# Decay matrices two slots ahead in three buffers, and four further changes to the state-space stage of a hybrid diffusion backbone

## What is computed

```python
z, xs, B, C, dt = proj(h)                     # xs, B, C through a 3-tap convolution and silu
# per group (8), per chunk of 128 tokens (10), for both directions:
decay = exp(where(tri, a_cum[l] - a_cum[s], -inf))
y_diag = einsum((C @ B.T) * decay, x * dt)    # inside a chunk
state  = state * chunk_decay + B.T @ (decay_out * x * dt)
y_off  = exp(a_cum) * (C @ state_before)      # from the chunks before
y = (y_f + y_b + x * d_skip) * silu(z)
y = y * rsqrt(mean(y*y over the group) + eps) * norm_g
out = y @ w_out
```

## Time and profile before

| | |
|---|---|
| Median of 3 runs | 2400.05 us (2393.45 to 2405.62) |
| The profiled execution | 2396.67 us, span 2394.9 us |
| PE busy | 2136.1 us (89%) |
| DVE busy | 1425.8 us (60%) |
| ACT busy | 1131.6 us (47%) |
| POOL busy | 463.8 us (19%) |
| Granted TensorE clock, mean | 0.938 |
| `sg_rowb<-crows` DMAs | 80 of 512 KB, median 3.8 us from issue to landing |
| `h_wr<-in_w_ssd` DMAs | 48 of 512 KB, median 3.3 us |

### The profile page before, as it was taken

One profiled execution on the slowest core, in us unless ns is written; L12 is line 12 of the kernel. 1 busy time (PEld: TensorE's weight loads), 2 busy tenths in 40 slices (PEclk: granted clock), 3 DMA queues, 4 the chain that ended last, 5 costly groups with the idle time before them and its releaser, 6 DMA issues. The chain is left out here.

```text
span 2394.9 us, 35742 instructions
## 1 busy us (share of the span) xinstructions
PE 2136.1 (89%) x12490; PEld 1751.9 (73%) x12490; DVE 1425.8 (60%) x3348; ACT 1131.6 (47%) x2840; POOL 463.8 (19%) x449
## 2 busy tenths in 40 slices
PE   5699999899999989999876899569999999999787
PEld 2488777787877878787655788457778778877676
DVE  5475959778695977869395221433545554554652
ACT  5245647465563746556363111324444444444431
POOL 1013223232322323232120000111101111110300
PEclk9899999999999999999877999679999999999899
DMA  9423222131212213121126433321112111211432
GB/s 363 191 65 84 71 87 80 45 103 51 92 54 79 80 44 99 52 96 63 41 75 229 120 115 109 111 72 48 50 45 71 54 50 57 68 50 44 144 77 80
DMA packets 119645, 209.94 MB, mean 88 GB/s; under 512 B 28700, under 2 KB 78876, under 8 KB 117420
## 3 DMA queue, kind: packets, MB, share of 16 engines
q1 hardware_dynamic: 119468, 207.66, 27.1%
HBM read 180.93 MB, written 28.65 MB: 88 GB/s over the span
## 5 line engine op out<-in xcount | busy, mean ns | idle before, releaser
L546 PE MATMUL sg_pP<-h_h_hi,h_whi 128*128 128x512 f32 (+1 forms) x1152 | 438.6, 381 | 0.0
L547 PE MATMUL sg_pP<-h_h_lo,h_whi 128*128 128x512 f32 (+1 forms) x1152 | 415.6, 361 | 0.0
L548 PE MATMUL sg_pP<-h_h_hi,h_wlo 128*128 128x512 f32 (+1 forms) x1152 | 413.6, 359 | 0.0
L546 PE MATMUL at_pP<-h_h_hi,at_whi 128*128 128x512 f32 (+1 forms) x640 | 253.9, 397 | 12.8 <-POOL at_wlo L2084 12.8
L546 PEld LDWEIGHTS sg_pP<-h_h_hi,h_whi 128*128 128x128 f32 x1152 | 226.2, 196 | 30.6 <-issue 0.2
L547 PEld LDWEIGHTS sg_pP<-h_h_lo,h_whi 128*128 128x128 f32 x1152 | 225.8, 196 | 30.4
L548 PEld LDWEIGHTS sg_pP<-h_h_hi,h_wlo 128*128 128x128 f32 x1152 | 224.3, 195 | 32.2
L548 PE MATMUL at_pP<-h_h_hi,at_wlo 128*128 128x512 f32 (+1 forms) x640 | 238.6, 373 | 0.0
L547 PE MATMUL at_pP<-h_h_lo,at_whi 128*128 128x512 f32 (+1 forms) x640 | 237.0, 370 | 0.0
L967 ACT ACTIVATE sg_S<-sg_rowb,sg_tab 128x128 f32<-128x128 f32 x640 | 195.7, 391 | 47.8 <-DVE sg_E L1229 47.8
L2084 POOL TENSOR_TENSOR at_wlo<-at_wr,at_whi 128x1024 fp32r<-128x1024 f32 x32 | 76.3, 2385 | 564.3 <-ACT at_whi L1959 564.3
(11 more groups left out here) (293 smaller groups left out, 4595.4 us busy)
## 6 DMA issues: line engine op xcount, KB each, us to landing
sg_rowb<-crows SPq DMA_DIRECT2D x80, 512.0 KB, 3.8
h_wr<-in_w_ssd SPq DMA_DIRECT2D x48, 512.0 KB, 3.3
fs_w<-in_ada_w SPq DMA_DIRECT2D x16, 1024.0 KB, 8.8
at_wr<-in_w_na SPq DMA_DIRECT2D x32, 512.0 KB, 3.5
at_bias<-bt SPq DMA_DIRECT2D x256, 64.0 KB, 2.3
op_yr<-y SPq DMA_DIRECT2D x10, 1024.0 KB, 7.7
fs_w<-in_ada_w SPq DMA_DIRECT2D x16, 512.0 KB, 8.6
y<-sg_Z SPq DMA_DIRECT2D x16, 512.0 KB, 3.0
```

The lines of the kernel that those rows point to most:

```text
L546: pe.matmul(out, w_hi[:, k, :], h_hi[:, k, t0:t0 + n], start=(k == 0), stop=False)
L547: pe.matmul(out, w_hi[:, k, :], h_lo[:, k, t0:t0 + n], start=False, stop=False)
L548: x = pe.matmul(out, w_lo[:, k, :], h_hi[:, k, t0:t0 + n], start=False, stop=(k == KT - 1))
```

## The change

1. C B^T goes into a bank of its own (`pA[1]`), and DVE makes both masked copies of it from PSUM in the backward slot of the chunk (`masks`, into `cbl` and `cbg`). ACT's copy into `cb` and DVE's `triangles` in later slots are gone.
2. `norm_g` is no longer multiplied onto y in `norm_early` but onto the output weights in `out_project`, in the two instructions that split them; the last step of the norm is one multiplication over both tiles.
3. PE makes `back(g + 1, 0)` in slot 19 of group g, ahead of `forth_inner`; in a slot from 2 on without a unit, `back_state` is put off until behind the next `back`. DVE's `norm_late` in slots 0 and 1 stands ahead of `back`.
4. `rowb` has one buffer instead of two (and so one semaphore, `rld`); the cumulative rows `cumt` are kept in `hb`, `bias` and `alog` in `sq`. A broadcast waits for the `segments` of the chunk before, and the lists of broadcasts are cut otherwise: chunk 0 alone, 1 to 3, 4 to 6, 7 to 9 instead of 0 and 1, 2 to 4, 5 to 7, 8 and 9.
5. `E` has three buffers, and `forward_part`, `masked`, `times_decay` and `decays` work on chunk c + 2 instead of c + 1, `segments` and `nearer` on chunk c + 3 instead of c + 2.

```diff
@@ SP
             def rows(g, chunks):
                 for c in chunks:
                     n = g * NCH + c
-                    if n >= 2:
-                        sp.wait_ge(sgs, n - 1)
+                    if n:
+                        sp.wait_ge(sgs, n)
                     else:
                         sp.wait_ge(rst, 16 * 2 * G)
-                    sp.dma_start(rowb[:, n % 2, :, :].rearrange("p h l -> p (h l)"),
-                                 rows_dram[g, c].rearrange("h l -> (h l)").partition_broadcast(P)
-                                 ).then_inc(rld[n % 2], 16)
+                    sp.dma_start(rowb[:, :, :].rearrange("p h l -> p (h l)"),
+                                 rows_dram[g, c].rearrange("h l -> (h l)").partition_broadcast(P)).then_inc(rld, 16)
...
                 if kind == "x" and g and i:
-                    rows(g - 1, ((0, 1), (2, 3, 4), (5, 6, 7))[i - 1])
+                    rows(g - 1, ((0,), (1, 2, 3), (4, 5, 6))[i - 1])
                 if kind == "x" and g >= 2 and i == 0:
-                    rows(g - 2, (8, 9))
+                    rows(g - 2, (7, 8, 9))
                 if kind == "x" and g == G - 1 and i == XT - 1:
-                    rows(g - 1, (8, 9))
+                    rows(g - 1, (7, 8, 9))
@@ PE
+                if n:
+                    pe.wait_ge(msk, n)
+                pe.matmul(pA[1][:, 0:P], X[:, g % 2, B_, u0:u0 + P], X[:, g % 2, C_, u0:u0 + P],
+                          start=True, stop=True).then_inc(tC, 1)
                 for t in range(XT - 1):
-                    pe.transpose(pT[:, t * P:(t + 1) * P], X[:, g % 2, t, u0:u0 + P], ident[:, :])
-                pe.matmul(pT[:, 3 * P:4 * P], X[:, g % 2, B_, u0:u0 + P], X[:, g % 2, C_, u0:u0 + P],
-                          start=True, stop=True).then_inc(tA, 1)
+                    x = pe.transpose(pT[:, t * P:(t + 1) * P], X[:, g % 2, t, u0:u0 + P], ident[:, :])
+                x.then_inc(tA, 1)
...
+            back(0, 0)
             for g in range(G):
+                behind = None
                 for i in range(NCH):
-                    back(g, i)
+                    if i:
+                        back(g, i)
+                    if behind is not None:
+                        back_state(g, behind)
+                        behind = None
                     if units[g][i] is not None:
                         unit(units[g][i])
-                    if i < NCH - 1:
+                    elif 2 <= i < NCH - 1:
+                        behind = i
+                    if i < NCH - 1 and behind is None:
                         back_state(g, i)
...
+                    if c == NCH - 1 and g + 1 < G:
+                        back(g + 1, 0)
                     forth_inner(g, c)
@@ ACT
-                    if -1 <= c < NCH - 1:
-                        forward_part(g, c + 1)
                     if -2 <= c < NCH - 2:
-                        segments(g, c + 2)
-                    if -1 <= c < NCH - 1:
-                        decays(g, c + 1)
+                        forward_part(g, c + 2)
+                    if -3 <= c < NCH - 3:
+                        segments(g, c + 3)
+                    if -2 <= c < NCH - 2:
+                        decays(g, c + 2)
@@ DVE
-                if g == 0 and nxt == 3:
+                if g == 0 and nxt == 8:
+                    dve.wait_ge(rst, 16 * 2 * G)
                     dve.wait_ge(tst, 32)
...
-            def triangles(g, c):
...
+            def masks(g, i):
+
+                n = g * NCH + i
+                dve.wait_ge(tC, n + 1)
+                if g and i == 0:
+                    dve.wait_ge(wfw, g * NCH)
+                dve.tensor_tensor(cbg[:, BACK[i], :], pA[1][:, 0:P], ge[:, :], ALU.mult)
+                dve.tensor_tensor(cbl[:, BACK[i], :], pA[1][:, 0:P], le[:, :], ALU.mult).then_inc(msk, 1)
...
-                    for t in range(PAIRS):
-                        zt = Z[:, t, (c - 3) * P:(c - 2) * P]
-                        x = dve.scalar_tensor_tensor(zt, zt, ng[:, g * PAIRS + t:g * PAIRS + t + 1],
-                                                     norm_bank(c - 1)[:, P:2 * P], ALU.mult, ALU.mult)
-                    x.then_inc(fin, 1)
+                    zc = Z[:, :, (c - 3) * P:(c - 2) * P]
+                    dve.tensor_tensor(zc, norm_bank(c - 1)[:, P:2 * P].unsqueeze(1).to_broadcast([P, PAIRS, P]), zc,
+                                      ALU.mult).then_inc(fin, 1)
...
+                    if g and s < 2:
+                        norm_late(g - 1, NCH + s)
                     if c >= 0:
                         norm_early(g, c)
                     if c < 0:
+                        masks(g, s)
                         back(g, s)
                     else:
                         offs(g, c)
                         scan(g, c)
-                    if g and s < 2:
-                        norm_late(g - 1, NCH + s)
                     if c >= 0:
                         norm_late(g, c)
-                    if -1 <= c < NCH - 1:
-                        masked(g, c + 1)
-                        times_decay(g, c + 1)
                     if -2 <= c < NCH - 2:
-                        triangles(g, c + 2)
+                        masked(g, c + 2)
+                        times_decay(g, c + 2)
...
-                    if -2 <= c < NCH - 2:
-                        nearer(g, c + 2)
+                    if -3 <= c < NCH - 3:
+                        nearer(g, c + 3)
@@ out_project, for each of the 16 weight tiles (and a load of ng ahead of them)
+                    act.activation(whi[:, k, :], wr[:, k % RW, :], ACT.Copy, scale=ng[:, k:k + 1]).then_inc(whs, 1)
...
+                    dve.scalar_tensor_tensor(wlo[:, k, :], wr[:, k % RW, :], ng[:, k:k + 1],
+                                             whi[:, k, :].bitcast(F32), ALU.mult, ALU.subtract).then_inc(wls, 1)
```

More of the change, by code:

```diff
@@ L618, in ssd_groups @@
         diag = m.sb("diag", [P, P])
-        rowb = m.sb("rowb", [P, 2, H8, P])
+        rowb = m.sb("rowb", [P, H8, P])
         S = m.sb("S", [P, H8, P])
-        E = m.sb("E", [P, 2, HPG, P])
+        E = m.sb("E", [P, 3, HPG, P])
         W = m.sb("W", [P, HPG, P])
@@ L638, in ssd_groups @@
         ecum, dec, dtdec, ncum = tv, te, tu, tq
-        cumt = rowb[0:H2, :, :, :].rearrange("p i h l -> p (i h l)")[:, 0:TOK]
+        cumt = hb[0:H2, :, :].rearrange("p c n -> p (c n)")[:, 4 * UN:4 * UN + TOK]
         GT = TABS * NCH * H8
@@ L698, in _ @@
             load(1)
-            for dst, src in ((par, "conv"), (ng, "norm_g"), (ident, "ident"), (le, "m_le"),
+            for dst, src in ((par, "conv"), (ident, "ident"), (le, "m_le"),
                              (ge, "m_ge")):
@@ L858, in norms @@
                     x.then_inc(ssm, 1)
-            pe.wait_ge(small, 128)
+            pe.wait_ge(small, 112)
             for c in range(NCH):
@@ L966, in segments @@
                 for k in range(H8):
-                    x = act.activation(S[:, k, :], rowb[:, n % 2, k, :], ACT.Identity,
+                    x = act.activation(S[:, k, :], rowb[:, k, :], ACT.Identity,
                                        bias=tab[:, g % 2, NCUM, c, k:k + 1])
@@ L976, in back @@
                 act.activation(X[:, g % 2, 0:XT - 1, u0:u0 + P], pT[:, 0:3 * P].rearrange("p (t c) -> p t c", c=P),
[L977 to L981, removed]
+                               ACT.Copy).then_inc(evA, 1)
             def forward_part(g, c):
                 n = g * NCH + c
-                act.wait_ge(tri, 2 * n + 2)
+                act.wait_ge(msk, masks_of(g, c))
                 if n:
@@ L989, in forward_part @@
                 for k in range(HPG):
-                    x = act.activation(W[:, k, :], cb[:, c, :], ACT.Copy, scale=tab[:, g % 2, DT, c, k:k + 1])
+                    x = act.activation(W[:, k, :], cbl[:, c, :], ACT.Copy, scale=tab[:, g % 2, DT, c, k:k + 1])
                 x.then_inc(wfw, 1)
@@ L995, in decays @@
                 act.wait_ge(mns, n + 1)
-                act.activation(E[:, n % 2, :, :], E[:, n % 2, :, :], ACT.Exp).then_inc(ex, 1)
+                act.activation(E[:, n % 3, :, :], E[:, n % 3, :, :], ACT.Exp).then_inc(ex, 1)
             def square(g, c):
@@ L1081, in _ @@
             pool.wait_ge(con, 5)
-            pool.wait_ge(small, 128)
+            pool.wait_ge(small, 112)
             def scaled(slot, g, c, lo):
@@ L1144, in _ @@
             dve.memset(hz, 0.0).then_inc(con, 1)
-            dve.wait_ge(small, 128)
+            dve.wait_ge(small, 112)
             dve.wait_ge(ttr, 1)
@@ L1395, in _, with out_project @@
                 norm_late(G - 1, c)
-def out_project(nc, a, layer, y_dram, kt, w_dram, tiles, mod_rows, st_o, runs=None):
+def out_project(nc, a, layer, y_dram, kt, w_dram, tiles, mod_rows, st_o, runs=None, scale=None):
     NH = D // 2
@@ L1426, in out_project @@
         N = len(tiles)
+        if scale is not None:
+            ng = m.sb("ng", [P, kt])
+            ngl = m.sem("ngl")
         if runs:
```

(11 more changed lines are left out.)

48 lines of the change are left out of this document (22 added, 26 removed).

## The result

The changed kernel takes **2454.98 us** (median of 4 runs, 2449.44 to 2467.41), the kernel before 2398.28 (4 runs, 2393.45 to 2405.62): ratio 1.024, 95% interval 1.0199 to 1.0281. It is slower, as forecast (2450, range 2405 to 2485). The profiled execution of after took 2459.85 us at a span of 2458.1; before it was 2396.67 at 2394.9. So 63.2 us of span are to be explained.

A forecast was written before the change was run, and what follows sets the result against it. DVE bounds the forward half, PE the backward half. Group 0 +25, groups 1 to 5 +7.0 each, group 6 +2, group 7 -9, output stage +0.5: +53.5 us on 2396.7, so 2450 us, range 2405 to 2485.

The forecast's parts named there:

- The loop: Forward half, group 3: rows wait for segments, loads for ACT's split; PE 11.3 us late at slot 12.
- The cause: Row transfers through the single `rowb` buffer: segments follow segments no faster than 6.2 us.
- Group 0: Eight gather DMAs between load and broadcasts cost 5.3 us three times, 16; with the rest +25 us (17 to 29).
- Slot 3: Backward half: the state product, put off, waits for DVE's masks; between 1.4 us won and 1 lost, taken as 0.6 lost.
- Group 7: No loads in its forward half, slots near 6.2 us; backward half gives 3; -9 us (-11 to -6).
- the steps moved out and the last slots: Group 7's forward half: a gain of 3 us, beside 3.1 from shorter slots.
- What follows the stage: Output stage: 16 splits with a scalar operand and a small load added, +0.5 us (0 to 2).
- (a): Rival: the stall never reaches PE and DVE's relief counts in full, 2335 us; 8%.
- (b): Rival: lateness of the first three broadcasts is absorbed, stalls in slots 11 and 14 remain, 3.7 us each; 2384 us; 10%.
- (c): Rival: PE's lower clock spreads, two to four more slow slots in each of eight groups; 2476 to 2501 us; 10%.
- What was to show it: Profile signs: ACT waits for rows, PE for `sq`, DVE for decays; `L837`'s 39 us mostly go; forward halves 88 to 92.

The follow-up runs named there:

- e1: The changed kernel with the row transfers behind the weight loads in the lists of before (0-1, 2-4, 5-7, 8-9): 2356.62 us, 0.9817 to the kernel before.
- e4: The changed kernel with the extra slot of lead taken back on ACT and DVE, its new lists and one buffer kept: 2354.83 us, 0.9811.
- e2: The changed kernel with two buffers of rows instead of one, masks held in bfloat16, its new lists kept: 2474.84 us, 1.0311.
- e3: The changed kernel with the output stage's strided gathers moved behind the row transfers in SP's list: 2439.56 us, 1.0162.
- e5: e1 with DVE making the masks of backward slot 3 ahead of the convolution and gate of slot 2: 2339.12 us, 0.9761.
- e7: The changed kernel with both the old lists and the old lead, single buffer and all else kept: 2342.81 us, 0.9781.
- e13: The changed kernel with chunk 1's row transfer moved behind the earlier weight load (lists 0-1, 2-3, 4-6, 7-9): 2429.12 us, 1.0131.

## Why the prediction was right, and where it was wrong

**The sum.** Span against span, each group up to the end of its slot 19, as the forecast counts it:

| | forecast | measured |
|---|---|---|
| group 0 | +25 (17 to 29) | +25.2 |
| groups 1 to 5, each | +7.0 (2.0 to 9.5) | +8.9 |
| group 6 | +2 (-1 to +6) | +3.8 |
| group 7 | -9 (-11 to -6) | -6.4 |
| what follows | +0.5 (0 to 2) | -4.0 |
| start of group 0 | 0 | +0.2 |
| total | +53.5 | +63.2 |

So 9.4 us of the difference lie in groups 1 to 5, and 4.5 of the opposite sign behind the stage, where the forecast had nothing of the kind. The medians are 56.7 apart and the profiled executions 63.2. That 2450 came within 5 us of the median is in part luck; the range isn't.

**The loop: right, step by step.** From the load of slot 8 in group 3, forecast and measured: S(3) ends at 19.5 and 19.4; the next load goes at 24.5 and 24.4; B(4) lands at 29.7 and 29.0 (landing 4.1, not the 4.8 of the earlier trace rows); the square ends at 33.5 and 32.8; slot 12 starts at 33.9 and 33.7, so PE is 11.1 us late where I had 11.3. Slot 15 starts at 62.8, not 59.1, 13.1 late, where the sum took 11.8: slot 12 ran at a clock of 0.75 and took 11.44 us where I allowed up to 10.3, and everything behind it moved. Slots 15 to 19 took 38.2 us up to the end of slot 19 (forecast 35.8 to 38.5), so 3.4 us came back where the sum took 4.2. In groups 1 to 5 slots 15 to 19 took 38.2 to 39.4.

**The cause: half right.** I began the mechanism with "`rowb` has one buffer now". As a pace it holds: S follows S after 6.1 us inside a list of after (688.07 to 694.15). As the cause it is refuted: e1 and e4 keep the one buffer and have no stall, e2 has two and keeps it. It takes the new order of the rows and the new lead together; take back either and 98 to 100 us go. What stands of the step is the rest of its paragraph: the first row of a list behind a load, wanted by ACT in that load's own slot, and ACT's split, for which the next load waits, queued behind it.

**Group 0: right.** The group is 25.2 us longer. The gathers' 16 us were measured at 14.3 (e3, group 0), having given the 5.3 us each.

**Slot 3: the wait right, its price too small.** PE waits 2.73 us for the masks, where it waited 1.95 for `xdb`; the 0.6 lost that I took implied about that. But slots 3 and 4 together take 9.5 us instead of 8.3 in the mean of groups 1 to 6: 1.2 lost, over my bound of 1, and 2.0 in group 3 (10.58 instead of 8.58), the worst. There slot 4 stretched from 5.37 us at a granted clock of 0.68 to 7.14 at 0.57. I had costed idle time and not the clock behind it. e5 returned it and more.

**Group 7: the forward half mis-sized by 4.** The backward half won 4.2 us (49.3 instead of 53.5, up to slot 10) where I had 3; 0.65 of it is `back(7, 0)`, now done in group 6. The forward half won 2.2 us (65.7 to DVE's last norm multiplication, 67.9 before) where I had 6.1. Slots 13 to 18 are near 5.9 us, a little below the 6.2 of the forecast, and won 4.0 together. But slots 10 to 12 took 21.0 us instead of 18.4, and for that the forecast had no term; "the steps moved out and the last slots", 3 us, had no row behind them. Slot 12 before and after:

```profile
1212.63:1218.37 5.74, 5.37 (x26) 3.77 (x26) 5.44 (x15) 4.44 (x14) 2.01 (x3) 0.66 0.17 49
```

```profile
1284.08:1290.42 6.34, 6.25 (x26) 4.78 (x26) 4.62 (x13) 3.61 (x12) 2.00 (x3) 0.50 0.28 90
```

The same products kept PE busy for 6.25 us at a granted clock of 0.50, half of full speed, where it was 5.37 at 0.66. Why slots 10 and 11 got longer by 2.0 us stays open.

**What follows the stage: -4.0**, against +0.5. e1 has the same output stage as after and ends 1126.2 us behind DVE's last norm multiplication, after 1123.0, before 1127.0. So 3 us of it vary without any change to that stage, and no effect is shown.

**The rivals.** (a) is refuted, PE did stall; but its figure for a kernel without the stall, 2335, is nearly what e7 (2343) reaches. Where PE doesn't stall, a forward half of group 3 takes 78.6 us (e1) or 77.5 (e7) instead of 82.4, with the next `back` in it, so most of the relief of DVE does count. (b) has the first lateness absorbed. It isn't: with the first list's border put right, e13 is 4.7 us a group shorter. (c) is right in kind: between e1 and after 34 of 85 us in groups 1 to 6 are clock. It ran beside the forecast, not in its place; against before PE's busy time rose by 12.5.

**What was to show it.** ACT's wait for rows, PE's for `sq`, DVE's for the decays: all there. The forward halves of groups 1 to 5 take 92.2 to 93.6 us up to the end of slot 19, at and above the upper end of the 88 to 92; 0.65 of it is the next group's `back`. That of group 0 is the longest, as said, at 108.1. Not there: `L837`'s 39.2 us "mostly go", but 34.4 stayed as `L841`'s, 2.71 of it in the stalled slot 10 of group 3. In e4, without stalls, it is 25.2.

## What to carry to other kernels

A transfer that shares an in-order queue with others has a slack of its own: the time from when the entry ahead of it can go to when it is wanted. Before deepening a pipeline by a slot, write that slack down for the first transfer of every list; here one slot (6 to 9 us) covered a landing of 4.3 us, but not landing and gathers together, and none covered neither. A second buffer helps only where the buffer is what the transfer waits for.

## What the runs showed of the hardware

The long stalls of TensorE are paid twice here. Slot 12 of after, without any idle time of PE, took 11.44 us at a granted clock of 0.75, behind 6.60 us of idle time in the slot before; in e1, where 0.97 us of idle time lie in the slot before, it takes 8.68 at 1.00:

```profile
649.96:658.64 8.68, 8.68 (x50) 7.10 (x50) 8.33 (x21) 7.09 (x18) 1.86 (x3) 1.00 0.33 113
```

Two row transfers (512 KB each) issued together behind a load landed 5.2 and 5.9 us after issue, one alone 4.3. The masks read from PSUM were cheaper than I had them, not dearer. Two of 128 columns with no wait between them occupy DVE for 0.40 us (start to start of what follows), where the pair of triangles, with a wait between them, took 0.53. DVE in e1, group 4:

```profile
725.71 0.28 DVE L1229 TENSOR_TENSOR sg_cbg<-sg_pA,sg_ge 128x128 f32<-128x128 f32 x1
725.91 0.28 DVE L1230 TENSOR_TENSOR sg_cbl<-sg_pA,sg_le 128x128 f32<-128x128 f32 x1
726.11 0.42 DVE L1218 TENSOR_TENSOR sg_hb<-sg_hb,sg_tab 128x256 f32<-128x256 f32 x1
```
